# GLA gate logits: one stacked product of 48 rows in place of an fp32 product of 16 rows

## What is computed

```python
z = h @ w_in
(..., a_low, ...) = jnp.split(z, points, axis=-1)      # a_low: 16 columns per token
log_a = jax.nn.log_sigmoid((a_low @ w_gate_up + b_gate).astype(jnp.float32)) / GLA_GATE_TAU
```

## Time and profile before

| | us |
|---|---|
| median of 3 runs | 2156.66 |
| lowest, highest | 2154.49, 2161.83 |
| the profiled execution's own time | 2155.36 |
| its span in the profile | 2153.7 |
| TensorE busy (share of the span) | 2065.1 (96%) |
| VectorE, ScalarE, GpSimd busy | 1040.6, 629.6, 313.8 |
| mean granted TensorE clock | 0.979 of full speed |

### The profile page before, as it was taken

One profiled execution on the slowest core, in us unless ns is written; L12 is line 12 of the kernel. 1 busy time (PEld: TensorE's weight loads), 2 busy tenths in 40 slices (PEclk: granted clock), 3 DMA queues, 4 the chain that ended last, 5 costly groups with the idle time before them and its releaser, 6 DMA issues.

```text
span 2153.7 us, 31138 instructions
## 1 busy us (share of the span) xinstructions
PE 2065.1 (96%) x12125; PEld 1853.0 (86%) x12125; DVE 1040.6 (48%) x2210; ACT 629.6 (29%) x1124; POOL 313.8 (15%) x317
## 2 busy tenths in 40 slices
PE   7799998999999999999889999999999999999996
PEld 6589998999999786787689977998898889989995
DVE  4599993345454330555654425344433442343345
ACT  5333212322333451455443213212121112121212
POOL 3133223332313121000034210000000000000000
PEclk9899999999999999999989999999999999999998
DMA  5122332222212242444634231111101110111002
GB/s 157 35 77 82 120 100 80 82 88 70 70 51 85 72 132 91 153 145 150 233 111 137 75 134 35 45 59 59 40 24 56 59 40 20 59 60 40 20 1 91
DMA packets 143915, 174.34 MB, mean 81 GB/s; under 512 B 9464, under 2 KB 120734, under 8 KB 143262
## 3 DMA queue, kind: packets, MB, share of 16 engines
q1 hardware_dynamic: 136446, 148.66, 21.3%
q0 software_dynamic: 7328, 23.67, 3.1%
HBM read 127.90 MB, written 44.40 MB: 80 GB/s over the span
## 4 chain that ended last, share of the span: by engine, by line
PE 46%; DVE 2%; DMA 1%; issue 1%; ACT 0%; POOL 0%; DVEq 0%; SPq 0%; ACTq 0%; POOLq 0%
PE ring L880 15%; PE ring L881 15%; PE ring L882 15%; DVE arena L2293 0%; DVE arena L2248 0%; PE ring L875 0%; DMA od_whole<-dsa_outputs 0%; DVE z_lo L2172 0%; DMA piece_whole<-w_gla_branch 0%; PE ring L1181 0%; ACT od_hi L1599 0%; DMA arena<-g_final 0%; DVE z_whole L2199 0%; DVE arena L2158 0%; POOL piece_lo L2309 0%
## 5 line engine op out<-in xcount | busy, mean ns | idle before, releaser
L880 PE MATMUL ring<-n_hi,piece_hi 128*128 128x352 f32 (+1 forms) x1320 | 438.4, 332 | 0.9 <-DVE n_lo L1767 0.7
L882 PE MATMUL ring<-n_hi,piece_lo 128*128 128x352 f32 (+1 forms) x1320 | 426.4, 323 | 0.0
L881 PE MATMUL ring<-n_lo,piece_hi 128*128 128x352 f32 (+1 forms) x1320 | 425.8, 323 | 0.0
L1279 ACT ACTIVATE arena<-ring 128x352 f32<-128x352 f32 (+8 forms) x368 | 153.1, 438 | 465.6 <-PE ring L882 333.1
L880 PEld LDWEIGHTS ring<-n_hi,piece_hi 128*128 128x128 f32 (+1 forms) x1320 | 249.3, 189 | 10.2 <-issue 7.5
L881 PEld LDWEIGHTS ring<-n_lo,piece_hi 128*128 128x128 f32 (+1 forms) x1320 | 249.6, 189 | 0.4
L882 PEld LDWEIGHTS ring<-n_hi,piece_lo 128*128 128x128 f32 (+1 forms) x1320 | 248.6, 188 | 0.3
L2309 POOL TENSOR_TENSOR piece_lo<-piece_whole,piece_hi 128x1024 fp32r<-128x1024 f32 (+2 forms) x52 | 118.5, 2278 | 562.7 <-ACT piece_hi L1292 562.5
L1854 DVE TENSOR_SCALAR_CACHE_REDUCE arena<-arena 128x384 uint8<-128x384 f32 (+6 forms) x224 | 190.6, 874 | 1.4 <-DVE arena L1854 0.2
L881 PE MATMUL ring<-h_lo,gate_hi 128*128 128x352 f32 x528 | 170.9, 324 | 7.6 <-issue 7.6
L880 PE MATMUL ring<-h_hi,gate_hi 128*128 128x352 f32 x528 | 172.0, 326 | 0.0
(11 more groups left out here) (283 smaller groups left out, 3638.1 us busy)
## 6 DMA issues: line engine op xcount, KB each, us to landing
piece_whole<-w_in SPq DMA_DIRECT2D x54, 512.0 KB, 3.7
projected_rows<-arena SPq DMA_DIRECT2D x44, 528.0 KB, 2.7
arena<-projected_rows SPq DMA_DIRECT2D x12, 1056.0 KB, 5.5
gate_whole<-w_ffn_gate SPq DMA_DIRECT2D x11, 1024.0 KB, 5.2
up_whole<-w_ffn_up SPq DMA_DIRECT2D x11, 1024.0 KB, 5.2
down_whole<-w_ffn_down SPq DMA_DIRECT2D x11, 1024.0 KB, 4.8
arena<-projected_rows SPq DMA_DIRECT2D x16, 528.0 KB, 3.6
arena<-x_prompt SPq DMA_DIRECT2D x16, 512.0 KB, 6.3
```

What stands on the lines that cost most here:

```text
L880: pe.matmul(out, lhi, rhi, start=first, stop=False)
L881: pe.matmul(out, lhi, rlo, start=False, stop=False)
L882: return pe.matmul(out, llo, rhi, start=False, stop=last)
L1279: evacuates(act.activation(dst, src, ACT.Copy, scale=scale), *key)
```

## The change

Both operands of the gate product are split in halves and stacked along the contraction, in partitions 64 to 111: the 48 rows of the weights are (high, high, low), those of the activations (high, low, high). One matmul in F32R then sums high x high, high x low and low x high.

- ScalarE, at n = 3 behind the high half of piece 5, copies the high halves of `wgu` (16 x 512) and of `alT` (16 x 1056).
- GpSimd, at n = 3 behind the low half of piece 5 and ahead of the near bias loads, subtracts to get the two low halves, waiting for itself after each.
- SP, at n = 4 behind the load of piece 8, waits for both low halves and issues six small DMAs inside SBUF, 16 rows each, that build the two stacks.
- ScalarE waits for the stacks at the end of n = 6 (the halves of `alT` lie in the staging buffers), SP at n = 16, TensorE before the gate logits.
- `gate_logits` takes the stacks. Number, shape and order of the products and of their evacuations stay.

```diff
+        al_hi, al_lo = halves("al_hi", o_sg, T)[IDM:IDM + RANK, :], halves("al_lo", o_sg + T, T)[IDM:IDM + RANK, :]
+        al3 = halves("al_stack", ARENA - T, T)[IDM:IDM + 3 * RANK, :]
+        assert n32 >= GH * GDK + 8
+        gu3 = halves("gate_up_stack", -(-o_c32 // 8) * 8, GH * GDK)[IDM:IDM + 3 * RANK, :]
...
-        relx = at(region(DH * P), DH, P)
+        top[0] += -top[0] % 8
+        o_rx = region(DH * P)
+        relx = at(o_rx, DH, P)
+        gu_hi, gu_lo = (halves(f"gate_up_{k}", o_rx + i * GH * GDK, GH * GDK)[IDM:IDM + RANK, :]
+                        for i, k in enumerate(("hi", "lo")))
...
                 load(n + 4)
+                if n == 4:
+                    sp.wait_ge(al_lo_done, 2)
+                    for k, (g_, a_) in enumerate(((gu_hi, al_hi), (gu_hi, al_lo), (gu_lo, al_hi))):
+                        sp.dma_start(gu3[RANK * k:RANK * (k + 1), :].bitcast(F32), g_.bitcast(F32)).then_inc(stack_in, 16)
+                        sp.dma_start(al3[RANK * k:RANK * (k + 1), :].bitcast(F32), a_.bitcast(F32)).then_inc(stack_in, 16)
                 if n == C0 + 1:
+                    sp.wait_ge(stack_in, 96)
...
-                    done(pe.matmul(ps[:, 0:W3], wgu[:, h * GDK:(h + 1) * GDK],
-                                   alT[:, n * W3:(n + 1) * W3], start=True, stop=True), "gz", h, n)
-
+                    done(pe.matmul(ps[:, 0:W3], gu3[:, h * GDK:(h + 1) * GDK],
+                                   al3[:, n * W3:(n + 1) * W3], start=True, stop=True), "gz", h, n)
+
+            pe.wait_ge(stack_in, 96)
...
                     hi_piece(n + 2)
+                if n == 3:
+                    act.activation(gu_hi, wgu, ACT.Copy).then_inc(al_hi_done, 1)
+                    act.activation(al_hi, alT, ACT.Copy).then_inc(al_hi_done, 1)
+                if n == V0 - 1:
+                    act.wait_ge(stack_in, 96)
...
                 if n == 3:
+                    g.wait_ge(al_hi_done, 2)
+                    g.wait_ge(p_lo_done, n + 3)
+                    g.tensor_tensor(gu_lo, wgu, gu_hi, ALU.subtract).then_inc(al_lo_done, 1)
+                    g.wait_ge(al_lo_done, 1)
+                    g.tensor_tensor(al_lo, alT, al_hi, ALU.subtract).then_inc(al_lo_done, 1)
+                    g.wait_ge(al_lo_done, 2)
+                if n == 3:
```

More of the change, by code:

```diff
@@ L595, in build @@
         relb_in = sem("relb_in")
+        al_hi_done, al_lo_done, stack_in = sem("al_hi_done"), sem("al_lo_done"), sem("stack_in")
         grow_in, pagetab_in, one_set = sem("grow_in"), sem("pagetab_in"), sem("one_set")
```

## The result

The changed kernel is faster: median 2144.15 us of six runs (2140.65 to 2145.51) against 2157.11 us for six runs of the kernel before (2153.97 to 2161.83). The ratio is 0.9937 with a 95% interval of 0.9922 to 0.9952, some 13.6 us (13.0 between the two medians). The forecast was 2152.2, its range ended at 2148.5, and "faster" had a chance of 0.13: the prediction was wrong. The profiled execution took 2143.39 us (span 2141.7), against 2155.36 (span 2153.7) before: 12.0 us between the spans.

The account below looks back on a forecast made before the run. TensorE, busy for 96% of the span, was taken to bound the kernel. The products were to save 4.5 us, splitting 0 and stacking 0, taking the median from 2156.66 to 2152.2 us, range 2148.5 to 2157.5.

Parts of the forecast that it names:

- Nothing after 729 has a start of its own, so I carry the shift through to the end in full: Everything behind the gate products: the time saved there, 4.5 us, was claimed to reach the kernel's end undiminished.
- Below nothing: nothing here frees an engine: Splitting and stacking ahead of the products: forecast 0, with no gain possible below that.
- The gate stretch: Twelve gate products up to transposes and dense group: one record each instead of two, forecast to save 4.5 us.
- ScalarE frees a bank every 0.58 us: Gate stretch: ScalarE's evacuations, 0.58 us each, were claimed to set the pace, the 9th ending at 735.2.
- the 0.284 of the prediction: Gate products before the change: 0.284 us per weight load at full clock, so 0.57 us per two-record product.
- earlier: Before the page transposes: VectorE's sample queries and bias table claimed finished at 734.14, ahead of the transposes' start at 735.2.
- the case of no fall: Gate stretch rival: the clock never falls, gain 6.0 us, 2150.7 us; chance 0.10.
- the slower rival: First two page pairs: the clock stays down beyond the first dense group, 3.8 us slower, 2160.5 us; chance 0.05.
- The early part: Splitting and stacking from piece 5 on: claimed hidden, cost 0; rival that it leaks, up to 3.8 us, chance 0.06.
- The cover: Slack behind the added splitting work before the engine's next work: 0.7 us on ScalarE; GpSimd loads end 144.0, next work 144.49.
- over 9: VectorE's idle before the attention: a sign of being right was that it stays over 9 us.
- the rivals of the gate stretch: Clock never falls, 2150.7 us, chance 0.10; clock late for the whole dense group, 2154.4 us, chance 0.16.

Follow-up runs that it names:

- after_mm6: Changed kernel with six tiny fp32 products (24 instructions) added at the head of TensorE's program; 2151.55 us, ratio 0.9972 to the kernel before.
- late_half: Changed kernel with half of each gate product's columns evacuated and TensorE's two waits for VectorE moved behind the page transposes; 2142.09 us, one execution.
- split_fp32: Changed kernel with the gate product back in fp32 over 16 rows, splitting, stacking and waits kept; 2159.83 us, ratio 1.0005 to the kernel before.

## Why the prediction was wrong

**"Nothing after 729 has a start of its own, so I carry the shift through to the end in full", and "Below nothing: nothing here frees an engine".** This is the step that failed. The pauses behind the jumps have their length by the place of the loop in the stream, and the change takes 24 loads and matmuls out from ahead of it and adds a wait. That gave 6.3 us, and no term and no rival held it. What showed it was in the trace of the kernel before, in the waits of TensorE over the feed-forward stage: three idle times of some 2.5 us with "issue" as their releaser, on the engine that is busy for 96% of the span. The prediction looked at no wait behind 769. The second failure of the same step is the fall at 773.9: shifted work met the clock differently, and 1.7 us did not cost what they had. Both were gains, and both can go the other way: after_mm6 is the changed kernel with the loop back near its old place and has pauses of 6.4 us, and late_half is faster at the gate and has the fall.

The Trainium skill (Runtime: NRT & Kernel Launch, section on instruction fetch mechanics) says that an engine's instructions are fetched ahead in blocks, in sequence, and that a taken branch to a target outside what is held must fetch before it can go on. The traces agree in kind: a stop behind a jump back, 2.5 to 3.5 us from the last matmul ahead of it to the resumption, at a fixed place in the stream. That the place of the loop's head decides how much of that is hidden, from 6.4 to 7.7 us down to none per three jumps, is what the runs add. The fetch itself is in no row here, so that it is the cause of the stop remains the page's explanation; shown is only the dependence on the number of instructions ahead.

**The gate stretch: forecast 4.5, measured 4.7 in this pair of profiles.** The size was right by two errors that met:
- "ScalarE frees a bank every 0.58 us" was wrong. The 0.58 of the earlier trace rows was TensorE's own pace at full clock, which the evacuations followed: two records with starts 0.296 us apart (the 0.284 of the prediction divides the length of 14 loads by 14). That the two were equal should have warned me. Freed of it, evacuations start 0.44 us apart, and the transposes began 5.1 us after the first product, not 6.0: 5.7 us earlier than before, where 4.8 was forecast. VectorE's table, called "earlier", is last by a hair.
- The clock came back 5.4 us after the transposes began, not 3.1 to 4.4. The stretch from the transposes to the scores took 7.3 us rather than 6.3, which gave 1.0 back.

**The one profile was a cheap sample.** In two of four fp32 profiles the stretch to the scores took 20.5 us, not 17.1; against those the gain is 8.1. I took 10.88 us for the price of the products though it hung on the moment when the clock fell (14.1 with the early fall), and no term of the sum let that moment vary. Nor do the runs bear out that it was the 16 rows that did not hold the clock: it falls 0.3 to 0.5 or 3.5 to 3.7 us after the first product, in two and two of the fp32 profiles and in three and seven of the stacked ones. In the 17 us ahead of the first product TensorE was busy for 12.9, the same in both kernels. What sets the moment stays open.

**Right were:** one record per product, twelve in all. The clock fell in this stretch too, so the case of no fall was rightly a small one, and it was back before the dense group ended, so the slower rival did not come. Against the rule of the Trainium skill on psum-queue depth-cycling (TensorE: Matmul & The Clock Gate): the trace agrees that the clock falls while the banks are cycled, but one fall and one return are all there is in this stretch, and the loss was 1.0 us. The early part was hidden as worked out. ScalarE's timeline in the kernel after:

```profile
130.95 0.63 ACT L1458 ACTIVATE gate_up_hi<-arena 16x512 fp32r<-16x512 f32 x1
131.48 1.07 ACT L1459 ACTIVATE al_hi<-arena 16x1056 fp32r<-16x1056 f32 x1
133.23 0.47 ACT L1295 ACTIVATE arena<-ring 128x352 f32<-128x352 f32 x1 [0.68 <-PE ring L897]
```

GpSimd's:

```profile
133.99 1.28 POOL L2380 TENSOR_TENSOR gate_up_lo<-arena,gate_up_hi 16x512 fp32r<-16x512 f32 x1
135.34 2.46 POOL L2382 TENSOR_TENSOR al_lo<-arena,al_hi 16x1056 fp32r<-16x1056 f32 x1
138.10 4.26 POOL L2388 DMA_DIRECT2D arena<-near_bias_rows  x8 [0.30 <-POOL al_lo L2382]
142.59 2.83 POOL L2328 TENSOR_TENSOR piece_lo<-piece_whole,piece_hi 128x256 fp32r<-128x256 f32 x4 [0.23 <-ACT piece_hi L1308]
```

The cover is 0.68 us on ScalarE (0.7 forecast) and 0.23 on GpSimd (0.5 forecast), and it held. The six issues on SP cost 0.58 to 0.60 us each instead of 0.37, 3.8 us together, with nothing waiting behind them. VectorE's wait before the attention is 12.59 us, where 13.05 stood in the earlier trace rows and "over 9" was expected.

**The range** reached 2148.5 by the rivals of the gate stretch alone. With the full price of what the profiles showed, 6.4 us for gate stretch and second fall and 6.3 for the loop, the time is 2157.1 - 12.7 = 2144.4; measured 2144.15. That the two are so close is in part luck: the 4.7 is the gain over the cheap sample, and medians move by 1 to 2 us.

## What to carry to other kernels

Before a shift is carried to the end, list every idle of the bounding engine, "issue" too. In this kernel the pause behind each back jump of a loop depends on how many instructions stand ahead of the loop, so any edit ahead of it can win or lose some microseconds, and a control that restores the count (here six tiny matmuls) parts that from the edit's own worth. Where an engine's period equals that of the engine that feeds it, it is not a price: work out which of the two sets it. A stretch whose length hangs on when the clock falls has no price from one profile; look at several executions.

## What was not expected of the hardware

- Three pauses behind back jumps of TensorE, 6.4 to 7.7 us in all with the loop where it stood or one instruction later, 1.8 to 2.6 with it 23 earlier, none with it 16 or 17 later. The stage moved by more than the pauses, 761.3, 755.0 and 751.0 us: behind the pause at 1920.84 the clock went to half as well (split_fp32 has such a fall behind each of its three pauses, and 765.2 us). Windows of the kernel before:

```profile
1924.00:1925.00 1.00, 1.00 (x6) 1.00 (x5) 0.98 (x1) 0.99 (x1) 0.00 (x0) 0.57 0.00 0
1925.00:1927.00 2.00, 2.00 (x9) 2.00 (x8) 1.32 (x1) 0.29 (x1) 0.00 (x0) 0.50 0.03 8
```

- The full clock was lost after 3.7 us of the fp32 products in one profile and after 0.3 in another, with TensorE busy all through them. It came back 3.1 to 3.5 us behind the start of the transposes in the fp32 profiles, 5.4 us in the kernel after.
- A fall of the clock worth 1.6 us at a place with the same waits in both kernels, which comes where the clock was back early in the stretch before, and not where it was back late.
- The profiles of the kernels before and after differ by 2 us before anything of the change runs. Their clocks rise and fall at different moments there: 0.9 us of it are there by 32 us, where the clock first rose at 26.3 in the one and at 24.4 in the other, and it goes from 0.8 to 2.0 with the half clock at 104.8 to 111.7 that only the kernel before has.
